# Two transformer blocks in one kernel: four of the six modulation vectors summed by POOL from two ring slots of their own, the in-projection on six slots, retention outputs finished tile by tile

## The chip, the cores and the metric

The kernel runs on one NeuronCore of a Trainium2 chip. The engines that matter are TensorE (PE, matrix products and transposes), VectorE (DVE), ScalarE (ACT), GpSimd (POOL) and SyncE (SP, which here issues weight loads). The metric is device microseconds of one launch, the median of several runs; lower is better.

## What is computed

Two blocks follow each other on 256 tokens of width 1024, everything in float32. The change touches the first one, and in it the vectors that modulate the norms, the projections and the retention heads:

```python
mod = silu(cond) @ w_mod + b_mod          # 1024 x 6144, six vectors of 1024 (shift1, scale1, gate1, shift2, scale2, gate2)
h  = rms_norm(x) * (1 + mod[1]) + mod[0]
hc = rms_norm(ctx) * (1 + mod_c[1]) + mod_c[0]
rq, rk, rv, rg, dq, dk, dv = split(h @ w_in)            # and the same of hc for keys and values
ret  = rms_norm(retention(rq, rk, rv)) * silu(rg)       # 4 heads, decaying scores
diff = rms_norm(differential_attention(dq, dk, dv))     # 4 heads, two softmaxes each
x  = x + mod[2] * (concat(ret, diff) @ w_out)
h2 = rms_norm(x) * (1 + mod[4]) + mod[3]
x  = x + mod[5] * peer_ffn(h2)   # per token 8 x 16 of 16384 experts are looked up and gathered
```

Only the first two vectors are needed for the context too (`mod_c`). The other four are needed for the latent tokens alone. The second block (block attention, a gated delta rule, a mixture of experts) comes behind all of this and is not changed.

## The kernel before

One function, `two_blocks`, writes a program for each engine by hand, with semaphores between them. All weights of the first block come in chunks of 1 MB (128 partitions x 2048 floats, seen as 8 feature blocks `k` of 256 columns) through a ring `wring` of 8 slots. Chunk `n` lives in slot `n % 8`; SP issues its load as soon as chunk `n - 8` was used (`chunk_used`), strictly in the order of `n`. The order of the stream is: 8 chunks of modulation vectors 0 and 1 (4 chunks for each vector), 12 of the in-projection, 12 of the vectors 2 to 4, then 4 of the out-projection (with those of vector 5 in between), 9 of the peer queries and their keys. The first expert gathers follow.

What happens, in order:

- **In-projection.** PE works through 19 parts (`IN1_PARTS`, each 32 matmuls of `L2344` in the trace's count), because 7 of the 12 chunks are used for the latent and for the context tokens. From part 10 on (`HEADS_FROM`), `diff_heads(p)` puts one piece of the eight differential-attention heads ahead of each part: the transposed heads (`L2275`), two score products (`L2286`), the transposes of the softmaxed rows of the head before (`L637`), and the outputs of the one before that (`L2304`). For each head DVE takes the row maxima (`L1499`, `L1500`), ACT the exponentials (`L905`), and DVE combines the two softmaxes (`L1503`, `L1504`, `L1508`, the last one over 128x512). Between these DVE also writes the decay tables (`L1486` to `L1493`) and rotates queries and keys (`rope`, `L1455` to `L1465`). Ahead of head 0 and of head 4 PE waits for the semaphore `roped`, which DVE raises behind its rotations (`L1469`, `L1561`).
- **Modulation vectors 2 to 4.** For each vector `mod_products` (`L620`) multiplies four chunks by the silu of the condition: four groups of rows in PSUM, 64 matmuls. ACT copies the result to `mod_rows` (`L879`), `mod_turn` (`L630`) adds the four groups and turns the row into a column by 8 tiny matmuls, and DVE adds the bias (`modulation`, `L1363`). These stand between the retention work: `scores(h)` (`L2363`), the masked decay by DVE (`mask_scores`, `L1544`), `outputs(h)` (`L2375`), which writes both token tiles of a head and raises `ret_y`.
- **Norms and out-projection.** ACT squares the outputs of a tile (`ret_squares`, `L931`), takes a root (`L939`), DVE normalizes (`L1531` to `L1536`), PE transposes the tile (`turn_mixed`), `project_out(t)` (`L2414`, 128 matmuls) multiplies it with the four out-projection chunks, DVE adds the gated result to x (`add_mixed`, `L1599`). Tile 0 goes first; `project_out(1)` stands behind the first two peer queries. The vector 5 is multiplied on PE ahead of the first query.
- **Peer experts.** A query (`L2441`) and its key scores (`L2455`) give DVE 16 experts per head and token; POOL gathers their rows from HBM (`L787`, 256 gathers of 1 MB into a ring of 8 places `G`), DVE takes the dot products (`L1809`), PE adds the weighted rows (`weighted_rows`, `L2478`), which frees a place (`slot_used`). POOL has no other work ahead of the first gather. Its few tensor operations (`mask_level`, `L807`, and `L822` to `L831`) come in the second block.

## Time and profile before

| What | Value |
|---|---|
| three runs, us | 1366.46, 1367.21, 1372.5; median 1367.21 |
| span of the profiled execution, us | 1367.2 |
| PE busy | 1162.8 us, 85% of the span |
| DVE busy | 713.7 us, 52% |
| ACT busy | 392.0 us, 29% |
| POOL busy | 286.6 us, 21% |
| transfers | 446.79 MB, mean 327 GB/s |
| first gather starts | 269.16 us |

No own time of the profiled execution is listed beside its span. The span agrees with the median of the runs to 0.01 us, so sums made against the span can be read as sums against the median. The span falls into three stages: up to some 270 us the first block's attention, up to some 925 us the gathers, and then the second block.

### The profile page before, as it was taken

Reading aid. Unit: us, or ns where it says so; the run is one execution under the profiler, and the core shown is the slowest. Engines: PE = TensorE matmul, PEld = TensorE weight load, DVE = VectorE, ACT = ScalarE, POOL = GpSimd, SP = SyncE. Lnnn points to the kernel's source line nnn. Section 1 sums busy time; section 2 is a strip of 40 time slices with the busy share of each in tenths; the row PEclk is TensorE's granted clock in tenths of the full one; section 3 lists DMA queues with packets and bytes.
Section 4 is the critical chain, followed back from the end, with each engine's and each line's share of the span. In section 5 each row is a group of like instructions: output and inputs, shape, how many; then the busy total and the mean of one; then the engine's idle time right before and its main releaser. Section 6 shows DMA issues by size and latency. Waiting matters only on the chain.

```text
span 1367.2 us, 16345 instructions
## 1 busy us (share of the span) xinstructions
PE 1162.8 (85%) x5986; PEld 716.0 (52%) x5986; DVE 713.7 (52%) x1850; ACT 392.0 (29%) x1094; POOL 286.6 (21%) x275
## 2 busy tenths in 40 slices
PE   6999998989999987778777777778999998867896
PEld 4887877874555532223222223325978875332342
DVE  2365532487677777767777666644752515311112
ACT  2203532223333333333233334222531423000011
POOL 0000000024444444444444434440030000000000
PEclk9999999999999999999999999999999998999999
DMA  9711237399999999999999999997521474999996
GB/s 392 302 62 62 93 116 315 147 406 395 421 421 421 422 420 421 422 421 399 422 422 422 421 419 399 421 422 313 196 94 63 185 292 177 427 424 424 425 388 257
DMA packets 60283, 446.79 MB, mean 327 GB/s; under 512 B 6704, under 2 KB 7088, under 8 KB 10160
## 3 DMA queue, kind: packets, MB, share of 16 engines
q0 software_dynamic: 36864, 268.45, 47.5%
q1 hardware_dynamic: 22912, 175.97, 31.8%
q10 hardware_dynamic: 432, 1.40, 0.3%
q8 instruction: 44, 0.72, 0.2%
q14 instruction: 31, 0.25, 0.0%
HBM read 444.74 MB, written 1.05 MB: 326 GB/s over the span
## 4 chain that ended last, share of the span: by engine, by line
PE 52%; DMA 34%; DVE 6%; ACT 4%; issue 2%; SPq 0%; POOL 0%; DVEq 0%; ACTq 0%
DMA arena<-uv_in,arena 26%; PE bank L2478 12%; PE bank L2344 9%; DMA wring<-moe_in 4%; PE bank L2575 4%; PE bank L2821 3%; PE bank L2441 3%; PE bank L2837 2%; DMA wring<-stream_in 2%; DVE arena L1809 2%; PE bank L2780 2%; DMA arena<-moe_in 2%; PE bank L2572 2%; PE bank L2807 2%; PE bank L637 1%
## 5 line engine op out<-in xcount | busy, mean ns | idle before, releaser
L2478 PE MATMUL bank<-arena 128*128 128x512 f32 x1024 | 474.1, 606 | 116.9 <-ACT arena L1069 116.9
L1809 DVE CUSTOM_DVE_ANT_0 arena<-arena 128x1024 f32<-128x1024 f32 x256 | 314.0, 1226 | 192.5 <-DMA arena<-uv_in,arena 191.5
L787 POOL DMA_INDIRECT arena<-uv_in,arena x256 | 272.0, 1063 | 650.1 <-PE bank L2478 365.7
L2478 PEld LDWEIGHTS bank<-arena 128*128 128x128 f32 x1024 | 186.6, 191 | 374.3 <-ACT arena L1069 192.7
L1061 ACT ACTIVATE arena<-arena 128x2 f32<-128x2 f32 x128 | 26.2, 205 | 410.0 <-DVE arena L1809 409.8
L2344 PE MATMUL bank<-wring,arena 128*128 128x256 f32 x608 | 134.1, 381 | 1.0 <-DVE arena L1384 1.0
L2344 PEld LDWEIGHTS bank<-wring,arena 128*128 128x128 f32 x608 | 115.2, 191 | 17.7 <-DVE arena L1384 1.1
L1069 ACT ACTIVATE arena<-const,arena 128x128 f32<-128x128 f32 x256 | 86.7, 385 | 0.0
L2441 PEld LDWEIGHTS bank<-arena,wring 128*128 128x128 f32 x384 | 57.0, 196 | 20.2 <-issue 15.3
L2821 PE MATMUL bank<-arena 128*32 128x512 f32 x288 | 59.7, 616 | 7.5 <-DMA arena<-moe_in 4.9
L2821 PE MATMUL bank<-wring,arena 128*32 128x512 f32 x288 | 59.7, 620 | 7.2 <-DMA wring<-moe_in 7.2
L2441 PE MATMUL bank<-arena,wring 128*128 128x128 f32 (+1 forms) x384 | 63.4, 314 | 1.8 <-DMA wring<-stream_in 1.8
L1065 ACT ACTIVATE arena<-arena 128x1 f32<-128x1 f32 x256 | 61.4, 287 | 4.2
L2575 PE MATMUL bank<-arena,wring 128*128 128x256 f32 x256 | 57.3, 381 | 0.0
L2575 PEld LDWEIGHTS bank<-arena,wring 128*128 128x128 f32 x256 | 48.0, 190 | 7.2 <-issue 0.8
L2162 DVE TENSOR_TENSOR arena<-bank,arena 128x256 f32<-128x256 f32 x9 | 3.8, 425 | 89.3 <-ACT arena L1294 89.3
L2837 PE MATMUL bank<-arena 128*32 128x512 f32 x184 | 34.6, 626 | 11.4 <-DMA wring<-moe_in 5.5
L2843 PE MATMUL bank<-arena 128*128 128x512 f32 x72 | 33.4, 604 | 8.6 <-DVE arena L2176 7.0
L2807 PEld LDWEIGHTS bank<-arena 128*128 128x128 f32 x288 | 34.8, 201 | 10.6 <-issue 8.0
L2807 PE MATMUL bank<-arena 128*128 128x128 f32 x288 | 36.3, 287 | 4.1 <-DVE arena L2064 4.1
L960 ACT ACTIVATE arena<-bank 128x512 f32<-128x512 f32 x19 | 11.3, 597 | 93.7 <-PE bank L2344 93.7
L620 PE MATMUL bank<-wring,tiny 128*32 128x256 f32 x384 | 26.2, 423 | 10.3 <-DMA wring<-stream_in 10.3
(458 smaller groups left out, 1318.5 us busy)
## 6 DMA issues: line engine op xcount, KB each, us to landing
wring<-stream_in SPq DMA_DIRECT2D x67, 1024.0 KB, 8.9
wring<-moe_in SPq DMA_DIRECT2D x14, 2048.0 KB, 17.9
arena<-moe_in SPq DMA_DIRECT2D x26, 1024.0 KB, 17.7
arena<-moe_in SPq DMA_DIRECT2D x12, 2048.0 KB, 18.7
wring<-moe_in SPq DMA_DIRECT2D x13, 1024.0 KB, 14.2
arena<-uv_in,arena POOLq DMA_INDIRECT x256, 12.8
arena<-moe_in SPq DMA_DIRECT2D x4, 512.0 KB, 10.7
wring<-moe_in SPq DMA_DIRECT2D x4, 512.0 KB, 11.2
```

The lines of the kernel that those rows point to most:

```text
L787: pool.indirect_dma_start(G[:, j, :], None, uv_d, src).then_inc(gathered[j], 16)
L1065: nc.scalar.activation(weight[:, at + q:at + q + 1], gelu[:, at + q:at + q + 1], ACT.Copy, scale=gates[:, first + q:first + q + 1]).then_i ...
L1069: nc.scalar.activation(diag[:, at + q, :], ident, ACT.Copy, scale=weight[:, at + q:at + q + 1]).then_inc(diag_ready, 1)
L1809: v.tensor_tensor_reduce(out=junk, in0=G[:, j, 0:D], in1=h2[:, t, :], scale=1.0, scalar=0.0, op0=ALU.mult, op1=ALU.add, accum_out=dots[:, ...
L2344: ins = mm(bank[1 + q % 2][:, t * COLS:(t + 1) * COLS], h[:, k, t * P:(t + 1) * P], w[:, k, :], start=k == 0, stop=k == KD - 1)
L2441: ins = mm(out[:, j, cols], w[:, k, j * P:(j + 1) * P], h2T[:, k, cols], start=k == 0, stop=k == KD - 1)
L2478: ins = mm(bank[1 + 2 * tile + c][:, :], diag[:, j, :], G[:, j, D + c * 512:D + (c + 1) * 512], start=False, stop=False, skip_group_check= ...
L2575: ins = mm(out[:, j * T:(j + 1) * T], w[:, k, j * P:(j + 1) * P], h3T[:, k, :], start=k == 0, stop=k == KD - 1)
L2807: ins = mm(bank[1 + k // 4][:, (k % 4) * P:(k % 4 + 1) * P], h4[:, t, k * P:(k + 1) * P], hotx[:, t], start=t == 0, stop=t == NT - 1)
L2821: ins = mm(bank[0][ROWS * j:ROWS * (j + 1), :], XT[:, k, ROWS * j:ROWS * (j + 1)], gu_buf(s)[:, k, :], start=k == 0, stop=k == KD - 1)
L2837: ins = mm(bank[1 + h][ROWS * j:ROWS * (j + 1), :], hidT[:, f, ROWS * j:ROWS * (j + 1)], home[:, f, h * 512:(h + 1) * 512], start=f == 0, ...
L2843: return mm(bank[4 + 2 * t + h][:, :], comb[:, t * P:(t + 1) * P], Yx[:, h * 512:(h + 1) * 512], start=False, stop=False, skip_group_check ...
```

## The change

The vectors 2 to 5 ("late" ones, 16 chunks) leave PE's products. POOL gets a loop ahead of its gathers: for each late chunk it multiplies 8x256 weights by the condition in place, and adds 4 blocks to 4, 2 to 2 and 1 to 1; the last addition writes 256 columns of `mod_rows`. PE only turns the row, with a matrix of ones, which sums over partitions too; the waits are on the new semaphore `pool_done`, raised four times for a chunk. The late chunks have slots 6 and 7 of the ring for themselves. The 12 in-projection chunks share slots 0 to 5, and the out-projection begins at slot 0 again. SP issues a late load behind certain in-projection loads (`LATE_MODS_AFTER`) and waits there for POOL, the last two behind the load of the keys.

On PE `mod_turn(2)` goes ahead of part 9, `mod_turn(3)` behind the fourth head's piece, `mod_turn(4)` behind the last part. DVE's `modulation(2)` moves ahead of the first `roped`, `modulation(3)` behind head 3's rows, `modulation(4)` ahead of the masked scores. The outputs of retention heads 2 and 3 are done for tile 0 first and then for tile 1. `project_out(1)` is cut into chunk 0, the sums of the norm, chunk 1, and later chunks 2 and 3, into banks 1 and 2; `clear(1)` and `clear(2)` now wait until DVE has read them.

```diff
+LATE_MODS_AFTER = {C_IN1 + 2: (0,), C_IN1 + 3: (1,), C_IN1 + 6: (2, 3), C_IN1 + 7: (4,), C_IN1 + 8: (5, 6),
+                   C_IN1 + 9: (7, 8), C_IN1 + 10: (9,), C_IN1 + 11: (10, 11, 12, 13), C_SK: (14, 15)}
@@ PE mod_turn
-            pe.wait_ge(mod_out, 2 * g + (1 if half == 0 else 2))
-            pe.wait_ge(cond_pick, 2)
+            if g < 2:
+                pe.wait_ge(mod_out, 2 * g + (1 if half == 0 else 2))
+                pe.wait_ge(cond_pick, 2)
+            else:
+                pe.wait_ge(pool_done, POOL_STEPS * MOD_GROUP * (g - 1))
@@ SP
+            def late_mod_in(m):
+                s = late_mod_slot(m)
+                if m < 2:
+                    sp.wait_ge(chunk_used, C_IN1 - 1 + m)
+                else:
+                    sp.wait_ge(pool_done, POOL_STEPS * (m - 1))
...
-                sp.wait_ge(chunk_used, n + 1 - WSLOTS)
+                if C_OUT1 <= n < C_IN2 and s >= IN1_SLOTS:
+                    sp.wait_ge(pool_done, POOL_STEPS * (LATE_MODS - WSLOTS + 1 + s))
+                else:
+                    sp.wait_ge(chunk_used, last_chunk_in(s, n) + 1)
@@ POOL, ahead of the gathers
+            for m in range(LATE_MODS):
+                g, n = 2 + m // MOD_GROUP, m % MOD_GROUP
+                w = slot_view(late_mod_slot(m))
+                pool.wait_ge(chunk_here[late_mod_slot(m)], 16 * (m // 2 + 2))
+                nc.gpsimd.tensor_tensor(w, w, bc(condS[:, :, 0], 2, COLS), ALU.mult).then_inc(pool_done, 1)
+                pool.wait_ge(pool_done, POOL_STEPS * m + 1)
+                nc.gpsimd.tensor_tensor(w[:, 0:4, :], w[:, 0:4, :], w[:, 4:8, :], ALU.add).then_inc(pool_done, 1)
+                pool.wait_ge(pool_done, POOL_STEPS * m + 2)
+                nc.gpsimd.tensor_tensor(w[:, 0:2, :], w[:, 0:2, :], w[:, 2:4, :], ALU.add).then_inc(pool_done, 1)
+                pool.wait_ge(pool_done, POOL_STEPS * m + 3)
+                if n == 0:
+                    pool.wait_ge(mod_turned, g + 1)
+                nc.gpsimd.tensor_tensor(mod_rows[:, n * COLS:(n + 1) * COLS], w[:, 0, :], w[:, 1, :], ALU.add)
@@ ACT
-            modulation_out(2, (6, 3))
-            modulation_out(3, (6, 3))
-            modulation_out(4, (1, 2))
-            modulation_out(5, (1, 2))
-                act.wait_ge(ret_y, RH)
+                act.wait_ge(ret_y, RH - 1 + t)
@@ PE, in-projection and retention
+                if q == HEADS_FROM - 1:
+                    mod_turn(pe, 2)
+                elif q == HEADS_FROM + 3:
+                    mod_turn(pe, 3)
...
-            mod_products(pe, 2, (6, 3))
-            outputs(0)
+            outputs(0).then_inc(ret_y, 1)
...
-            outputs(2)
-            mod_products(pe, 3, (6, 3))
-            outputs(3)
-            mod_turn(pe, 3)
-            mod_products(pe, 4, (1, 2))
+            outputs(2, (0,))
+            outputs(3, (0,)).then_inc(ret_y, 1)
+            outputs(2, (1,))
+            outputs(3, (1,)).then_inc(ret_y, 1)
...
-            mod_products(pe, 5, (1, 2), (0, 1))
+            project_out(1, (0,))
             sums_over_features(pe, sq2[0], 1, second=2)
-            mod_products(pe, 5, (1, 2), (2, 3))
+            project_out(1, (1,))
...
-            project_out(1)
+            project_out(1, (2, 3))
+            pe.wait_ge(x2_ready, 3)
             clear(1)
```

POOL before, at the head of its program; each row is one instruction or several alike, with the semaphores that it waits for:

```order
L783 UNCONDITIONAL_BRANCH [waits barrier_Pool_Activation_PE_DVE_SP_gather]
L787 DMA arena<-uv_in,arena 128x2048 [waits first_here]
L787 DMA arena<-uv_in,arena 128x2048 x7
L787 DMA arena<-uv_in,arena 128x2048 [waits slot_used,top_ready]
L787 DMA arena<-uv_in,arena 128x2048 [waits slot_used] x7
```

And after (the four tensor operations of the first chunk; 60 more follow ahead of the gathers):

```order
L832 UNCONDITIONAL_BRANCH [waits barrier_Pool_Activation_PE_DVE_SP_gather]
L843 ISA
L843 TENSOR_TENSOR wring<-wring,tiny 128x2048 [waits chunk_here6,inputs_ready]
L845 TENSOR_TENSOR wring<-wring 128x1024 [waits pool_done]
L847 TENSOR_TENSOR wring<-wring 128x512 [waits pool_done]
L851 TENSOR_TENSOR mod_rows<-wring 128x256 [waits mod_turned,pool_done]
```

The gathers now stand behind 64 tensor operations.

PE before, from the end of the in-projection (the last `L2344`) into the retention; `bank6<-wring,tiny` is `mod_products` of vector 2:

```order
L2344 MATMUL bank1<-wring,arena 128x256 x15
L2304 MATMUL bank7<-arena 128x128 [waits diff_aT_out]
L2304 MATMUL bank7<-arena 128x128 x3
L2363 MATMUL bank4<-arena 128x256 [waits proj_out,diff_exp,turned_out,const_here]
L2363 MATMUL bank4<-arena 128x256
L2363 MATMUL bank5<-arena 128x256 x2
L2363 MATMUL bank1<-arena 128x256 x2
L2363 MATMUL bank2<-arena 128x256 x2
L620 MATMUL bank6<-wring,tiny 32x256 [waits chunk_here4,diff_aT_out]
L620 MATMUL bank6<-wring,tiny 32x256 x7
```

And after, from the same place (`L664` is `mod_turn`, `L2442` are `outputs`):

```order
L2410 MATMUL bank1<-wring,arena 128x256 x15
L664 MATMUL bank3<-const,mod_rows 128x2 [waits pool_done,turned_out]
L664 MATMUL bank3<-const,mod_rows 128x2 x7
L2366 MATMUL bank7<-arena 128x128 [waits diff_aT_out]
L2366 MATMUL bank7<-arena 128x128 x3
L2430 MATMUL bank4<-arena 128x256 [waits diff_exp,proj_out,const_here]
L2430 MATMUL bank4<-arena 128x256
L2430 MATMUL bank5<-arena 128x256 x2
L2430 MATMUL bank1<-arena 128x256 x2
L2430 MATMUL bank2<-arena 128x256 x2
L2442 MATMUL bank0<-arena 128x128 [waits diff_y_out,ret_masked,diff_aT_out]
```

The products are gone and a turn stands in front.

DVE before, the rotation of the second tile and the first `roped`, on which PE's head 0 waits:

```order
L1455 TENSOR_TENSOR arena<-arena,const 128x1024 [waits dve_step]
L1462 TENSOR_TENSOR arena<-arena,const 128x32x16 x2
L1465 TENSOR_TENSOR arena<-arena 128x1024 [waits dve_step]
L1469 MEMSET tiny 128x128 [waits dve_step]
L1476 COPY arena<-bank 128x512 [waits turned] x2
```

And after (`L1424` is `modulation(2)`):

```order
L1516 TENSOR_TENSOR arena<-arena,const 128x1024 [waits dve_step]
L1523 TENSOR_TENSOR arena<-arena,const 128x32x16 x2
L1526 TENSOR_TENSOR arena<-arena 128x1024 [waits dve_step]
L1424 TENSOR_TENSOR tiny<-bank,small 128x16 [waits mod_turned,dve_step]
L1531 MEMSET tiny 128x128 [waits dve_step]
L1538 COPY arena<-bank 128x512 [waits turned] x2
```

One wait for PE's turn came in ahead of `roped`.

## Rows read from the trace of the kernel before

**Rows 1.** The page: DMA share of the span's 40 equal slices, in tenths.
```profile
DMA  9711237399999999999999999997521474999996
```
**Rows 2.** Chain that ended last, 0 to 360: start, duration, what.
```profile
221.53 9.04 DMA wring<-stream_in
...
249.72 4.89 DMA wring<-stream_in
```
**Rows 3.** Stretches: length, busy of PE, PEld, DVE, ACT, POOL, clock, DMA share, GB/s.
```profile
262.00:269.00 7.00, 6.48 (x58) 6.32 (x57) 6.38 (x33) 2.99 (x5) 0.00 (x0) 1.00 0.03 9
...
305.00:311.00 6.00, 4.57 (x14) 2.23 (x13) 5.79 (x18) 2.70 (x11) 2.37 (x2) 1.00 0.78 289
...
500.00:600.00 100.00, 73.70 (x160) 28.60 (x159) 69.72 (x178) 32.15 (x109) 41.02 (x40) 1.00 1.01 421
```
**Rows 4.** PE in order of time, 60 to 330: start, duration, line, idle before.
```profile
187.16 7.07 PE L2344 MATMUL bank<-wring,arena 128*128 128x256 f32 x32
...
197.98 3.66 PE L620 MATMUL bank<-wring,tiny 128*32 128x256 f32 x64
...
205.48 1.95 PE L630 MATMUL bank<-tiny,mod_rows 128*128 128x2 f32 x16
...
216.74 2.05 PE L2375 MATMUL bank<-arena 128*128 128x128 f32 x16
...
226.59 1.07 PE L637 MATMUL bank<-const,arena 128*128 128x128 f32 x8
230.71 17.08 PE L2414 MATMUL bank<-arena,wring 128*128 128x128 f32 x128 [3.05 <-DMA wring<-stream_in]
...
255.92 3.84 PE L2441 MATMUL bank<-arena,wring 128*128 128x128 f32 x32 [1.56 <-DMA wring<-stream_in]
...
267.00 14.46 PE L2414 MATMUL bank<-arena,wring 128*128 128x128 f32 x128
...
288.25 3.76 PE L608 MATMUL bank<-arena,const 128*128 128x128 f32 x16 [5.07 <-ACT arena L993]
```
**Rows 5.** DVE and POOL in order of time around 1011 to 1021.
```profile
1011.25 0.69 DVE L1917 TENSOR_TENSOR arena<-arena 128x512 f32<-128x512 f32 x1 [2.70 <-ACT arena L1188]
1011.29 1.77 POOL L807 TENSOR_TENSOR arena<-arena 128x512 f32<-128x512 f32 x1 [58.14 <-ACT arena L1188]
1012.04 1.57 DVE L1918 TENSOR_TENSOR arena<-arena 128x512 f32<-128x512 f32 x1
...
1014.78 1.90 POOL L822 TENSOR_TENSOR arena<-arena 128x1024 f32<-128x1024 f32 x1 [1.72 <-ACT arena L1196]
...
1018.59 0.42 DVE L1927 TENSOR_TENSOR arena<-arena,bank 128x256 f32<-128x256 f32 x1
...
1021.08 1.26 POOL L831 TENSOR_TENSOR arena<-arena 128x512 f32<-128x512 f32 x1
```
**Rows 6.** DVE in order of time: the two roped, one head's rows, one norm.
```profile
102.95 0.17 DVE L1469 MEMSET tiny<- 128x128 f32 x1
...
114.38 0.75 DVE L1508 SCALAR_TENSOR_TENSOR arena<-arena,tiny 128x512 f32<-128x512 f32 x1
...
144.13 0.17 DVE L1561 MEMSET tiny<- 128x128 f32 x1
...
222.62 0.69 DVE L1536 TENSOR_TENSOR arena<-arena 128x512 f32<-128x512 f32 x1
```
**Rows 7.** PE in order of time: where it needs those results of DVE.
```profile
105.32 1.04 PE L2275 MATMUL bank<-const,arena 128*128 128x128 f32 x8
...
119.41 0.66 PE L637 MATMUL bank<-const,arena 128*128 128x128 f32 x4
...
145.71 0.60 PE L2275 MATMUL bank<-const,arena 128*128 128x128 f32 x4
```
**Rows 8.** POOL in order of time: the first and the ninth gather.
```profile
269.16 1.12 POOL L787 DMA_INDIRECT arena<-uv_in,arena  x1 [268.73 <-DVE arena L1702]
...
299.12 0.96 POOL L787 DMA_INDIRECT arena<-uv_in,arena  x1 [20.15 <-PE bank L2478]
```

More of the change, by code:

```diff
@@ L46 @@
 C_IN1 = 2 * MOD_GROUP
-C_OUT1 = C_IN1 + N_IN1 + 4 * MOD_GROUP
+C_OUT1 = C_IN1 + N_IN1
 C_Q = C_OUT1 + N_OUT
@@ L50 @@
 C_IN2 = C_Q + N_Q + N_SK
-C_MOD = [0, MOD_GROUP] + [C_IN1 + N_IN1 + i * MOD_GROUP for i in range(4)]
+C_MOD = [0, MOD_GROUP]
 C_OUT2 = C_IN2 + N_IN2
@@ L55, with chunk_slot, late_mod_slot, chunk_turn @@
 WSLOTS = 8
+LATE_MODS = 4 * MOD_GROUP
+IN1_SLOTS = 6
+POOL_STEPS = 4
+MODS_SUMMED = POOL_STEPS * LATE_MODS
+def chunk_slot(n):
+    if C_IN1 <= n < C_OUT1:
+        return (n - C_IN1) % IN1_SLOTS
+    if C_OUT1 <= n < C_IN2:
+        return (n - C_OUT1) % WSLOTS
+    return n % WSLOTS
+def late_mod_slot(m):
+    return IN1_SLOTS + m % 2
+def chunk_turn(n):
+    late = LATE_MODS // 2 if n >= C_OUT1 and chunk_slot(n) >= IN1_SLOTS else 0
+    return late + sum(chunk_slot(m) == chunk_slot(n) for m in range(n + 1))
+LATE_MODS_AFTER = {C_IN1 + 2: (0,), C_IN1 + 3: (1,), C_IN1 + 6: (2, 3), C_IN1 + 7: (4,), C_IN1 + 8: (5, 6),
+                   C_IN1 + 9: (7, 8), C_IN1 + 10: (9,), C_IN1 + 11: (10, 11, 12, 13), C_SK: (14, 15)}
 SM = {}
@@ L185, in last_chunk_in @@
 def last_chunk_in(slot, before):
-    return max(n for n in range(before) if n % WSLOTS == slot)
+    return max(n for n in range(before) if chunk_slot(n) == slot)
 def two_blocks(nc, xT_d, ctxT_d, small_d, rows_d, const_d, masks_d, wstream_d, gate2_d, uv_d, route_d,
@@ L625, in mod_turn @@
         def mod_turn(pe, g, half=None):
[L627 to L628 removed]
+            if g < 2:
[3 more added lines that the diff above has]
+                pe.wait_ge(pool_done, POOL_STEPS * MOD_GROUP * (g - 1))
             for k in range(KD) if half is None else range(4 * half, 4 * half + 4):
                 ins = nc.tensor.matmul(bank[MOD_BANK[g] if half != 1 else 5][:, 2 * k:2 * k + 2],
[L631 removed]
+                                       mod_rows[:, k * P:(k + 1) * P], pick[:, 0:2] if g < 2 else ones[:, 0:2],
+                                       start=True, stop=True)
             ins.then_inc(mod_turned, 1)
@@ L787, in gather @@
                 pool.indirect_dma_start(G[:, j, :], None, uv_d, src).then_inc(gathered[j], 16)
+            pool.wait_ge(inputs_ready, 1)
+            for m in range(LATE_MODS):
[10 more added lines that the diff above has]
+                    pool.wait_ge(mod_turned, g + 1)
+                nc.gpsimd.tensor_tensor(mod_rows[:, n * COLS:(n + 1) * COLS], w[:, 0, :], w[:, 1, :], ALU.add)\
+                  .then_inc(pool_done, 1)
             pool.wait_ge(first_here, 1)
@@ L2349, in _ @@
                     ins.then_inc(chunk_used, 1)
+            pe.wait_ge(turned_out, len(sources))
+            mod_turn(pe, 4)
             diff_heads(DH * NT + 1)
             pe.wait_ge(const_here, 32)
-            pe.wait_ge(turned_out, len(sources))
             pe.wait_ge(proj_out, len(IN1_PARTS))
@@ L2365, in scores, with outputs @@
                 ins.then_inc(ret_scores, 1)
-            def outputs(h):
+            def outputs(h, tiles=range(NT)):
                 pe.wait_ge(ret_masked, h + 1)
@@ L2370, in outputs @@
                     pe.wait_ge(diff_y_out, NT)
-                for t in range(NT):
+                for t in tiles:
                     for k in range(4):
@@ L2404, in turn_mixed, with project_out @@
                         .then_inc(mixT_done, 1)
-            def project_out(t):
+            def project_out(t, chunks=range(N_OUT)):
                 pe.wait_ge(mixT_out, 2 * t + 2)
-                for n in range(N_OUT):
+                for n in chunks:
                     chunk_ready(pe, C_OUT1 + n)
```

59 lines of the change are left out of this document (29 added, 30 removed).

## The prediction, made before the changed kernel was run

> **What bounds the kernel now.** I read the page first. The DMA row of its slices is full from the eighth slice (some 270 us) to the twenty-seventh (some 925 us), and low before [rows 1]. The stretches say what that means: in 500 to 600 us the DMA share is 1.01 at 421 GB/s while PE idles a quarter of the time; just ahead of the first gather it is 0.03 [rows 3]. So the gather stage is a block of fixed length that is paid from the first gather on, at 269.16 us [rows 8], and the second block hangs behind it. What this change can move is the date of the first gather. Ahead of it the chain of waits is PE nearly throughout, with two pieces of weight loads: 9.04 us at 221.53 and 4.89 us at 249.72 [rows 2]. The PE timeline shows them as idle times of 3.05 and 1.56 us [rows 4]. POOL is idle all this time, 268.73 us ahead of its first gather [rows 8].
>
> **What goes away, part by part.** One group of products (64 matmuls) is 3.66 us, one turn 1.95 us [rows 4]. Three groups between 195 and 231 us go. Their turns do not go: two move into the in-projection, one to its end, so PE pays them there, less overlaps some 1.7 us each, 5 us together. Before, the retention from the end of the in-projection (187.16 + 7.07 = 194.2) to the last output (216.74 + 2.05 = 218.8) takes 24.6 us [rows 4], of which two groups and a turn are about 9.0. The rest, 15.6, stays. Since tile 0 is now finished first, its outputs end some 2 us earlier, and DVE's mask of head 3 is then about 0.5 late. So tile 0 is ready 5.0 + 15.6 - 2.0 + 0.5 = 19.1 us behind the old 194.2, at 213.3 instead of 218.8. From there the squares, the root and DVE's norm take as before: from 218.8 to 222.62 + 0.69 = 223.3 [rows 6], 4.5 us. PE turns the tile at 217.8 instead of 226.59, and the out-projection starts behind turn and copy (2.3 us) at 220.1 instead of 230.71: the 3.05 us of waiting for its weights are gone, since their loads are now issued during the in-projection. That is 10.6 us so far.
>
> Between the starts of `project_out(0)` and `query(0)` there were 25.2 us. Half a group of products twice (3.7) and the load wait of 1.56 go, two quarters of `project_out(1)` come in, each 14.46 / 4 = 3.6 [rows 4], and the first of them waits some 1 us for the copied tile. 25.2 - 5.2 + 7.2 + 1.0 = 28.2, so 3.0 us are given back, and a last 0.3 for the norm's row behind the later sums. The first gather comes 7.3 us earlier. Slots 6 and 7 don't delay the queries: with free engines the sixteenth late chunk is summed by about 225 us, and query 1 needs slot 6 some 20 us later.
>
> Behind the first gather DVE's selection for two heads sets `add_mixed(1)`; it shifts alike. New is that `clear` waits for it. The clears used to lie in a PE gap that ends with 5.07 us of waiting at 288.25, where the sums took 3.76 us instead of 2.05 [rows 4]. Now they and the sums start late together; I take 0.3 us. Two of the four query loads that ran beside the first gathers come earlier now, 2.1 MB or 5.0 us at 421 GB/s. I count nothing for it: the ninth gather is held by PE until 299.12 [rows 8], and the DMAs already have a hole behind it, share 0.78 in 305 to 311 [rows 3]. The hole gets larger instead; at most those 5 us are a gain. ACT's copies of the products go too; they hid beside PE and are worth nothing. **Without a cost of POOL's work: 1367.2 - 7.0 = 1360.2.**
>
> **What it adds.** No tensor operation of POOL runs in this stage before, so I bound it. The nearest rows: 1.26 us for two full operands of 512, 1.90 for 1024 with a broadcast factor [rows 5]. Doubling by size, a chunk is 3.8 + 2.5 + 1.3 + 0.6 = 8.2 us, and sixteen are 131 us. That fits between 38 us (first late chunk landed) and the gather at 262. The order that PE's turns impose splits it: chunks 0 to 4 from 38 to about 80, a pause until `mod_turn(2)` at 100 because `mod_rows` is still full, then 5 to 8, a short pause until `mod_turn(3)`, 9 to 12, a pause until `mod_turn(4)`, and 13 to 15.
>
> The question is what this does to DVE. In the only place where both read SBUF [rows 5], POOL's operation at 1011.29 took 1.77 us instead of 1.26, and DVE's at 1012.04 took 1.57 instead of 0.69, ending 0.55 us behind POOL's, about what its own data phase takes. That is full blocking in both directions, one behind the other. DVE's operation at 1018.59, which has one input in PSUM, ran its 0.42 us beside POOL unhindered. The Trainium skill (page "SBUF — State Buffer", section "Who interferes with whom") says this as a rule: a DVE instruction with two SBUF inputs and a GpSimd instruction that reads SBUF exclude each other for the whole instruction. It speaks against the change; by it the sum is the one below, and by a rule that shared the bandwidth instead it would be near the 1360 above.
>
> So each DVE operation with two SBUF inputs may wait for a whole POOL operation, 0.6 to 3.8 us, and POOL's next one then takes its turn ahead of DVE's next. In each head's part of 9 to 10 us DVE has 5 to 6 of them (`L1504`, `L1508`, the decay and rope lines), and PE leaves little room: `L1508` of head 0 ends at 115.1 and PE needs it at 119.41, 4.3 us; the second `roped` is at 144.3 and PE needs it at 145.71, 1.4 us; the first at 103.1 against 105.32, 2.2 us plus 1.7 of the inserted turn [rows 6, 7]. I walked through the parts, alternating the two engines:
> - first `roped`: POOL restarts at 100 with 0.6, 3.8, 2.5 us between DVE's last rope operations, and DVE arrives there some 2 us late; 113 against 107.4: 5.6 us.
> - heads 0 and 1: `L1504` and `L1508` wait behind 2.5 and 1.3 us, and the decay table of head 0 pushes the maxima of head 1: 0.3 and 3.2 us.
> - head 3 and the second rope, six operations beside chunk 9: `roped` 5.1 us late at head 4.
> - heads 4 and 5, decay sums and tables beside chunks 11 and 12: PE late by 3.0 and 2.1 us.
> - tail: the norm's product of tile 0 (`L1536`) meets chunk 13 or 14: 1.3 us.
>
> The sum is 20.6 us, beside 131 us of POOL work that could block at most. **1360.2 + 20.6 = 1380.8.** The lower end is 0, if every wait falls into slack; the upper end I take at 33, where chunk 1 also delays the context rows (`L1404`, 3 us of room there) and the three weak places come twice as bad.
>
> **The rivals.**
> - *The cover holds.* DVE is busy for hardly more than half of a part, POOL's pauses fall on its tight stretches, so PE never waits: 1360.2, down to 1357 if the two early loads count too. For it: POOL waits from about 80 to 100, just while DVE normalizes and rotates. Against it: 1.4 us of room at 145. This ends on the other side, and decides from the point where PE's added waits stay under 7 us. Chance 0.20.
> - *Half of it.* Blocking is real, but DVE's linked operations slip in before POOL's next one is issued, so a pair waits once instead of twice: some 10 us, 1370. Chance 0.22.
> - *POOL is late itself.* If an operation there took twice as long (262 us together), the turns and then the first gather would wait for POOL's chunk 15: chunks 13 to 15 alone would end 49 us after `mod_turn(4)`, near 252, still ahead of the gather, but `mod_turn(2)` and `mod_turn(3)` would hold PE some 10 and 20 us: 1390 and more. With everything above 1393: chance 0.08.
> - The forecast, blocking in alternation, 1372 to 1393: chance 0.50.
>
> The Trainium skill (page "GPSIMD Engine Reference", section "Performance versus the Vector engine") gives 4497 ns for an addition of 2048, where twice-doubled 1.26 us gives 5.0; the multiplication with its broadcast factor has no figure there. It would make a chunk about 8.4 us and change nothing above.
>
> **How the numbers follow.** The predicted time is the likeliest case's, 1380.5. The range 1359 to 1393 leaves out the low part of the first rival (under 0.10) and the 0.08 above. A measurement of this kernel can tell about 0.5% or 6.8 us from no change. Faster than 1360.4 is only a little more than half of the first rival: 0.13. Within 0.5%, up to 1374, are the rest of it, most of the half case and a little of the forecast: 0.30. Slower: 0.57.
>
> **What would show it.** Of the step on PE: no `L620` behind 195 us, no idle time for stream loads, and `project_out(0)` starting 23 to 25 us behind the end of the in-projection instead of 36.5. Of POOL: 8.2 us a chunk, pauses at the three turns, all done by 260. Of the blocking: `L1508`, `L1493` and the rope lines with means of 1.5 to 3 us instead of 0.4 to 0.75, PE idle behind DVE in front of the heads by some 19 us in sum, and the last part of the in-projection ending near 217 instead of 194. It would be wrong if those DVE means hardly rise, or if they rise and PE still runs through; then the gather starts near 262 instead of 282.

## The result, and the profile after

| | before | after |
|---|---|---|
| median of the runs | 1367.64 us (1366.46 to 1372.5) | 1391.58 us (1390.0 to 1393.06) |
| ratio after / before | | 1.0169, 95% interval 1.0143 to 1.0195 |
| span of the profiled execution | 1367.2 us | 1390.6 us |
| first gather starts | 269.16 us | 295.68 us |

The changed kernel is 24 us slower; 13.3 were forecast. The page of the changed kernel shows where. Its DMA row (40 slices of the span) is full from the eleventh slice on; the row of before was full from the ninth [rows 1]:

```profile
DMA  9723342268999999999999999997631364999996
```

The block of gathers has kept its length: from the first gather on there were 1367.2 - 269.16 = 1098.0 us before, and there are 1390.6 - 295.68 = 1094.9 now. So the loss, 26.5 us, lies wholly ahead of the first gather, and some 3 us come back behind it.

POOL in order of time (start, duration, engine, line; in brackets the idle time before it and what ended it): the four operations of the first late chunk, the three pauses that PE's turns impose, and the first gather. In the kernel before, that gather was the first thing POOL did [rows 8]:

```profile
43.55 3.62 POOL L843 TENSOR_TENSOR wring<-wring,tiny 128x2048 f32<-128x2048 f32 x1 [43.12 <-DMA wring<-stream_in]
47.25 2.35 POOL L845 TENSOR_TENSOR wring<-wring 128x1024 f32<-128x1024 f32 x1
49.68 1.26 POOL L847 TENSOR_TENSOR wring<-wring 128x512 f32<-128x512 f32 x1
51.02 2.65 POOL L851 TENSOR_TENSOR mod_rows<-wring 128x256 f32<-128x256 f32 x1
...
110.95 1.17 POOL L851 TENSOR_TENSOR mod_rows<-wring 128x256 f32<-128x256 f32 x1 [25.32 <-PE bank L664]
...
160.44 0.72 POOL L851 TENSOR_TENSOR mod_rows<-wring 128x256 f32<-128x256 f32 x1 [13.97 <-PE bank L664]
...
231.76 0.72 POOL L851 TENSOR_TENSOR mod_rows<-wring 128x256 f32<-128x256 f32 x1 [36.68 <-PE bank L664]
...
295.68 1.12 POOL L836 DMA_INDIRECT arena<-uv_in,arena  x1 [37.88 <-DVE arena L1764]
```

POOL is not late: it waits 76.0 us in three pauses for PE and 37.9 us for the gather's indices. VectorE (DVE) is late. Its groups of instructions between 20 and 300 us (line, shape, count, then busy time, mean of one in ns, and idle time before them):

```profile
L1445 DVE TENSOR_SCALAR arena<-arena,tiny 128x256 f32<-128x256 f32 x16 | 19.0, 1256 | 0.1
L1548 DVE TENSOR_SCALAR arena<-const,tiny 128x512 f32<-128x512 f32 x4 | 6.6, 1661 | 0.1
L1561 DVE TENSOR_REDUCE tiny<-bank 128x1 f32<-128x512 f32 x16 | 10.9, 683 | 8.9 <-PE bank L2348 8.9
L1570 DVE SCALAR_TENSOR_TENSOR arena<-arena,tiny 128x512 f32<-128x512 f32 x8 | 13.7, 1710 | 0.3
L1606 DVE SCALAR_TENSOR_TENSOR arena<-bank,arena 128x512 f32<-128x512 f32 x8 | 5.1, 685 | 6.7 <-PE bank L2430 6.7
```

and the same groups of the kernel before:

```profile
L1384 DVE TENSOR_SCALAR arena<-arena,tiny 128x256 f32<-128x256 f32 x16 | 5.4, 409 | 0.1
L1486 DVE TENSOR_SCALAR arena<-const,tiny 128x512 f32<-128x512 f32 x4 | 1.9, 484 | 0.1
L1499 DVE TENSOR_REDUCE tiny<-bank 128x1 f32<-128x512 f32 x16 | 11.0, 687 | 14.9 <-PE bank L2286 14.9
L1508 DVE SCALAR_TENSOR_TENSOR arena<-arena,tiny 128x512 f32<-128x512 f32 x8 | 6.0, 752 | 0.3
L1544 DVE SCALAR_TENSOR_TENSOR arena<-bank,arena 128x512 f32<-128x512 f32 x8 | 5.1, 684 | 3.5 <-PE bank L2363 3.5
```

The multiply-add of two SBUF tiles (`L1570`, before `L1508`) takes 1710 ns instead of 752. The forms that read PSUM (`bank`, `L1561` and `L1606`) are as they were: they are the control. But the scaling of the hidden rows (`L1445`) and the decay arguments (`L1548`) are three times as long too, and they have only one tile of SBUF as input, beside factors of one column each. The mean of 1256 ns still hides the size of it: eight of the sixteen scalings, those of the context rows, take 16.28 us together from 53.12 us on, and took 2.68 before; the other eight ran before POOL started and are unchanged.

What of this reaches PE stands in the table of its waits up to the first gather (line, releaser, sum, times, longest):

```profile
PE bank L651 <- DMA wring<-stream_in: 9.9, 3, 9.0
PE bank L2337 <- DVE tiny L1625: 7.3, 1, 7.3
PE bank L2410 <- DVE arena L1445: 6.4, 5, 2.9
PE bank L672 <- DVE arena L1570: 5.7, 2, 4.9
PE bank L672 <- DVE arena L1598: 4.8, 1, 4.8
PE bank L2348 <- ACT arena L970: 2.0, 1, 2.0
```

### The profile page after: what moved, and what is told of

It is laid out like the page before. It is cut to its first block, busy times and chain, and to the rows that moved or that the text cites. A ratio compares the mean times of both kernels' runs of the same rounds, so it can differ in the third digit from the quotient of the medians.

```text
span 1390.6 us, 15886 instructions
## 1 busy us (share of the span) xinstructions
PE 1163.1 (84%) x5730; PEld 712.0 (51%) x5730; DVE 783.6 (56%) x1850; ACT 388.3 (28%) x1086; POOL 426.6 (31%) x339
## 2 busy tenths in 40 slices
DMA packets 60282, 446.77 MB, mean 321 GB/s; under 512 B 6704, under 2 KB 7088, under 8 KB 10160
## 4 chain that ended last, share of the span: by engine, by line
PE 48%; DMA 33%; DVE 11%; ACT 5%; issue 3%; SPq 0%; DVEq 0%; ACTq 0%
DMA arena<-uv_in,arena 26%; PE bank L2538 12%; PE bank L2410 6%; PE bank L2881 4%; PE bank L2635 4%; DMA wring<-moe_in 4%; PE bank L2501 3%; PE bank L2840 2%; DVE arena L1871 2%; DMA wring<-stream_in 2%; PE bank L2897 2%; PE bank L2475 2%; DMA arena<-moe_in 2%; PE bank L2632 2%; PE bank L2867 1%
## 5 line engine op out<-in xcount | busy, mean ns | idle before, releaser
L2538 PE MATMUL bank<-arena 128*128 128x512 f32 x1024 | 478.5, 611 | 111.6 <-ACT arena L1130 111.1
L836 POOL DMA_INDIRECT arena<-uv_in,arena x256 | 277.2, 1083 | 412.8 <-PE bank L2538 363.6
L2410 PE MATMUL bank<-wring,arena 128*128 128x256 f32 x608 | 140.9, 391 | 7.2 <-DVE arena L1445 6.4
L843 POOL TENSOR_TENSOR wring<-wring,tiny 128x2048 f32<-128x2048 f32 x16 | 59.2, 3702 | 43.1 <-DMA wring<-stream_in 43.1
L845 POOL TENSOR_TENSOR wring<-wring 128x1024 f32<-128x1024 f32 x16 | 39.6, 2473 | 1.3
```

The costliest lines, as they stand in the source:

```text
L836: pool.indirect_dma_start(G[:, j, :], None, uv_d, src).then_inc(gathered[j], 16)
L843: nc.gpsimd.tensor_tensor(w, w, bc(condS[:, :, 0], 2, COLS), ALU.mult).then_inc(pool_done, 1)
L2410: ins = mm(bank[1 + q % 2][:, t * COLS:(t + 1) * COLS], h[:, k, t * P:(t + 1) * P], w[:, k, :], start=k == 0, stop=k == KD - 1)
L2538: ins = mm(bank[1 + 2 * tile + c][:, :], diag[:, j, :], G[:, j, D + c * 512:D + (c + 1) * 512], start=False, stop=False, skip_group_check= ...
```

## The experiments

Each kernel but one starts from the changed one. The date of the first gather is the measure in all of them: what follows it is of nearly fixed length, 1094.9 to 1099.4 us in the profiled execution of every kernel whose mixture of experts loads as much as before. The edits are shown in extracts: the signals (`.then_inc`) are left out, and so are most of the waits between POOL's steps.

**Without the sums.** Is it POOL's work, or the waits, slots and orders that came with it?

```
- nc.gpsimd.tensor_tensor(w, w, bc(condS[:, :, 0], 2, COLS), ALU.mult)
+ nc.gpsimd.memset(w[:, 0, 0:8], 0.0)
...
- nc.gpsimd.tensor_tensor(mod_rows[:, n * COLS:(n + 1) * COLS], w[:, 0, :], w[:, 1, :], ALU.add)
+ nc.gpsimd.memset(mod_rows[:, n * COLS:(n + 1) * COLS], 0.0)
```

> The changed kernel, but each of the 64 POOL operations that sum the sixteen late chunks (3.62, 2.35, 1.26 and 0.72 us) is replaced by a small memset that only writes (8 columns, the last one 256). Left out by this: the sums of modulation vectors 2 to 5, which become their bias alone. Kept: every load, every slot, every wait and semaphore, PE's turns, the order of SP, PE and VectorE. Theory A (VectorE's operations with both inputs in SBUF wait while POOL's sums run, nothing else of the change costs anything): this is the prediction's sum without POOL, 1360.2 us, within 1356 to 1364; project_out(0) starts at about 233 (255.6 in the changed kernel, 230.7 before less 10.6 plus what the first turn gives), the first gather near 262; the context rows' scaling (L1445) takes 0.41 us for 128x256 again, the head parts' multiply-add (L1570) 0.75 us. Rival B (the new waits and places - six slots, output tiles in another order, POOL's turn waits - cost the time): it stays between 1380 and 1392, the head parts as late as in the changed kernel.

Measured: first gather at 263.2 us, 32.5 earlier than in the changed kernel. The time, 1391.49 us, lies outside theory A's range, and does not show this: with other modulation vectors the tokens choose other experts in the second block's mixture, 453.06 MB are moved instead of 446.77, and the part behind the first gather takes 1127.6 us instead of 1094.9. So rival B's number came out and its mechanism did not. The scaling is at 410 ns again and the multiply-add at 752; taken by the date, the sums are the whole loss. (The expectation's 233 for `project_out(0)` was a slip: it starts at 222.42.) PE's stretch up to the first gather (length, busy with count for PE, PEld, DVE, ACT, POOL, granted clock, DMA share, GB/s), of the changed kernel and of this one:

```profile
0.00:295.68 295.68, 253.33 (x1436) 211.31 (x1437) 181.37 (x260) 74.69 (x152) 134.94 (x69) 0.93 0.45 177
```
```profile
0.00:263.20 263.20, 242.41 (x1436) 205.94 (x1437) 111.26 (x260) 74.06 (x152) 10.00 (x68) 0.97 0.49 198
```

Both hold the same 1436 matmuls. PE's idle time is 295.68 - 253.33 = 42.35 us in the one and 20.79 in the other: **21.6 us are waits**. The rest, 253.33 - 242.41 = **10.9 us, is the same work at a slower clock** (mean 0.93 instead of 0.97). It isn't POOL's traffic that slows the matmuls: from 75 to 86 us, at a granted clock of 1.00 and with POOL busy for 10.3 of the 11 us, the changed kernel runs 53 matmuls of 379 ns each, as many and as long as the kernel before with POOL idle. From 150 to 200 us, for example, of the changed kernel and of this one:

```profile
150.00:200.00 50.00, 40.69 (x202) 32.95 (x203) 36.36 (x38) 15.20 (x28) 33.77 (x16) 0.90 0.42 159
```
```profile
150.00:200.00 50.00, 49.20 (x262) 40.68 (x261) 22.28 (x48) 24.11 (x47) 0.94 (x8) 1.00 0.39 155
```

A mean of 0.90 is a mix of the clock's two levels, 2.4 and 1.2 GHz; where PE had stood idle for DVE it was granted the lower one for a part of the time.

**POOL busy, but only writing.** Seven memsets a chunk (two each of 2048, 1024 and 512 columns, one of 256), without a read:

```
- nc.gpsimd.tensor_tensor(w, w, bc(condS[:, :, 0], 2, COLS), ALU.mult)
...
+ for dst in (w, w, w[:, 0:4, :], w[:, 0:4, :], w[:, 0:2, :], w[:, 0:2, :]):
+     nc.gpsimd.memset(dst, 0.0)
+ nc.gpsimd.memset(mod_rows[:, n * COLS:(n + 1) * COLS], 0.0)
```

> The changed kernel, but POOL is kept as busy by seven memsets a chunk (twice 2048 columns, twice 1024, twice 512, once 256), which write SBUF and read nothing. Left out: the sums of modulation vectors 2 to 5, which become their bias. Same loads, slots and turns. Theory A1 (what holds VectorE up is POOL reading SBUF): VectorE's operations keep the durations of the kernel before (L1570 0.75 us, L1487 form 0.48, L1445 0.41) and the time is that of the kernel without sums, 1356 to 1364. Theory A2 (what holds it up is any POOL instruction under way): the same operations are as long as in the changed kernel wherever a memset runs, and the time lies above 1370, by as much as POOL's busy time per chunk comes to 8.2 us. Theory A3 (only the forms that an own port pair serves at a faster rate wait for a writer): the tensor_scalar forms (L1445, L1548) are longer, the tensor_tensor and multiply-add ones are not; then 1362 to 1370.

Measured: first gather at 259.8 us (and, with the same longer rest, 1389.83 us). The memsets keep POOL busy for 111.1 us up to the gather, a little less than the 134.9 of the sums. DVE's groups here; `L1441` is the hidden rows' scaling, `L1544` the decay arguments, `L1566` the multiply-add, `L1522` the addition of the rotation, `L1472` and `L1473` the small operations of the decay constants:

```profile
L1441 DVE TENSOR_SCALAR arena<-arena,tiny 128x256 f32<-128x256 f32 x16 | 10.6, 730 | 0.1
L1472 DVE TENSOR_TENSOR tiny<-tiny 128x8 f32<-128x8 f32 x7 | 1.2, 167 | 0.2
L1473 DVE TENSOR_SCALAR tiny<-tiny 128x8 f32<-128x8 f32 x7 | 6.5, 932 | 0.2
L1522 DVE TENSOR_TENSOR arena<-arena 128x512 f32<-128x512 f32 x2 | 1.4, 692 | 0.1
L1544 DVE TENSOR_SCALAR arena<-const,tiny 128x512 f32<-128x512 f32 x4 | 6.2, 1544 | 0.1
L1566 DVE SCALAR_TENSOR_TENSOR arena<-arena,tiny 128x512 f32<-128x512 f32 x8 | 6.0, 752 | 0.3
```

Theory A3 has the mechanism: while POOL only writes, the operations with two inputs run free, and the tensor_scalar forms still wait. Theory A1 has the date: a first gather no later than without POOL's work, so the waits of the tensor_scalar forms alone fall into slack here. The Trainium skill (page "SBUF — State Buffer", section "Who interferes with whom") has both: beside the two-input rule it says that `tensor_scalar` can enter a 2-port mode and then excludes GpSimd, and that a `tensor_reduce` never does on trn2. The trace agrees: the tensor_scalar of 512 columns, at 484 ns before faster than a tensor_tensor of the same size at 692, takes 1544 beside the memsets, and in the kernel below that starts its sums behind the context rows a tensor_reduce that reads 1024 columns of SBUF beside them keeps its 1.22 us.

**The same sums in pieces of 256 columns**, 15 operations a chunk instead of four:

```
+ for k in range(KD):
+     ins = nc.gpsimd.tensor_tensor(w[:, k, :], w[:, k, :], condS[:, k, 0:1].to_broadcast([P, COLS]), ALU.mult)
+ ins.then_inc(pool_done, 1)
```

> The changed kernel with the same sums, but POOL's operations are cut into pieces of 256 columns: 8 multiplies, 4 adds, 2 adds and 1 add a chunk instead of one of each; results and waits are the same. Theory A (a VectorE operation that meets a POOL operation waits until that one instruction has ended, then runs, then POOL waits for it in turn): the longest wait falls from 3.6 to at most 0.75 us, the mean of L1445, L1570, L1526 comes nearer to the kernel before (L1570 below 1.2 us), and 12 to 18 us of the 31 between the changed kernel and its cover come back: 1372 to 1379. Rival C (the two engines share the path in small turns, so what counts is the work that POOL does, not the length of its instructions): VectorE's means stay as they are, the time stays at 1385 to 1395 or above, as POOL's busy time grows by the fixed part of each instruction.

Measured: 1367.79 us, ratio to before 0.9998 (0.9976 to 1.002), first gather at 268.3. Theory A, and by more than it said (23.8 us came back, 12 to 18 were expected). POOL does more (180.8 us up to the gather instead of 134.9), and yet PE's idle time shrinks to 268.3 - 244.1 = 24.2 us, about that of the kernel without sums and one wait of 3.8, for the first rotated rows:

```profile
L1576 DVE SCALAR_TENSOR_TENSOR arena<-arena,tiny 128x512 f32<-128x512 f32 x8 | 9.3, 1168 | 0.3
```
```profile
PE bank L2343 <- DVE tiny L1537: 3.8, 1, 3.8
```

The multiply-add waits 0.42 us on average (1168 - 752) instead of 0.96: what a DVE operation pays is the rest of one POOL instruction, so the length of POOL's instructions counts and not their sum. Rival C, by which POOL's total would count, is out.

**The sums at other times.** POOL's chunk 0 waits for the decay constants, chunks 2 to 9 for one more finished head part each; turns, bias additions and loads follow later (`mod_turn(4)` behind the first mixed tile, and into another bank).

```
+ if m == 0: pool.wait_ge(gam_ready, 1)
+ elif 2 <= m < 10: pool.wait_ge(lam_dots, m)
- if q == HEADS_FROM - 1: mod_turn(pe, 2)
- elif q == HEADS_FROM + 3: mod_turn(pe, 3)
+ if q == HEADS_FROM + 3: mod_turn(pe, 2)
+ elif q == HEADS_FROM + 7: mod_turn(pe, 3)
```

> The changed kernel with the same sums at other times: POOL's chunk 0 waits until the decay constants are made (behind the context rows' scaling), chunks 2 to 9 wait each for one more head part of the eight to have ended on VectorE, PE's turns and VectorE's additions of the bias follow later (vector 2 in head part 3, vector 3 in head part 7, vector 4 behind the first mixed tile), and SP issues the later chunks' loads behind other weights. So the first eight sums spread out, and eight of the sixteen run behind the heads, where few VectorE operations have both inputs in SBUF. Theory A (collisions are the cost; fewer of them on PE's path give back the time): context rows at 0.41 us, head parts with at most one chunk each, 1366 to 1376. Rival D (moving the sums moves the collisions and adds waits at the turns): 1378 to 1392; PE would then stand idle in front of a turn (L664) or in front of the first mixed tile's use of vector 2.

Measured: 1364.03 us, ratio 0.9959 (0.9939 to 0.9979), first gather at 264.1. Theory A, a little better than its range. The same POOL instructions, 131.7 us of them, cost PE next to nothing:

```profile
0.00:264.10 264.10, 243.64 (x1436) 206.93 (x1437) 135.49 (x268) 74.50 (x152) 131.66 (x69) 0.97 0.51 198
```
```profile
L1574 DVE SCALAR_TENSOR_TENSOR arena<-arena,tiny 128x512 f32<-128x512 f32 x8 | 15.1, 1884 | 0.3
```

The multiply-add is even longer than in the changed kernel (1884 ns), and PE waits 0.3 us for it. The mean of a group says whether there is blocking, not whether it costs anything. The longest wait of PE for DVE is 3.1 us, in front of the mixed tile (2.7 without sums). Run again without an edit:

> The gated kernel once more, without any edit, against the kernel before, to narrow its interval. Expected: 1362 to 1366 us, ratio 0.995 to 0.998. If it was luck of one series, the ratio is 0.998 to 1.002.

Measured: 1365.62 us, ratio 0.9976 (0.9961 to 0.9992). Both intervals lie under 1, so the gain (0.41% and 0.24%) is likely real, but it is less than the 0.5% that the prediction took as the limit of what can be told.

**The start of the sums alone.** POOL waits until the last context row is scaled, and starts at 53.4 us instead of 43.6:

```
+ pool.wait_ge(h_ready, 2 * KD)
  for m in range(LATE_MODS):
```

> The changed kernel with one wait more: POOL's first sum starts when VectorE has scaled the last context row (near 60 us instead of 43.6). Everything else, the whole instructions of 2048, 1024, 512 and 256 columns too, stays. Theory A (each stretch of VectorE work pays for the POOL work that lies over it): the context rows come back to 0.41 us each and PE's waits for them (6.4 us in the changed kernel, 1.0 without sums) go, with part of the slower clock; POOL is then still at its chunks between 86 and 111 us, where it stood idle before, and its operations meet the normalising and rotating of the first rows, which ran free; that delays the first turned heads by 3 to 6 us. So the first gather comes 2 to 8 us earlier than the changed kernel's 295.7, at 288 to 294, and the time is 1384 to 1390. Rival E (the context rows are the root, and all the later waits follow from PE being late there): the first gather at 275 or earlier, the time under 1373.

Measured: 1406.18 us, ratio 1.0279 (1.0254 to 1.0304), first gather at 304.6: **later by 8.9 us**, where theory A gave 2 to 8 us earlier and rival E 20. Both were wrong. PE waits 1.0 us for the context rows, as hoped, and then

```profile
PE bank L2338 <- DVE tiny L1532: 26.1, 1, 26.1
```

for the first rotated rows. POOL's second chunk and then DVE in order of time show how they go in step; the small operations of the decay constants took 0.17 us each before:

```profile
61.62 3.62 POOL L844 TENSOR_TENSOR wring<-wring,tiny 128x2048 f32<-128x2048 f32 x1
65.31 2.36 POOL L846 TENSOR_TENSOR wring<-wring 128x1024 f32<-128x1024 f32 x1
67.75 1.28 POOL L848 TENSOR_TENSOR wring<-wring 128x512 f32<-128x512 f32 x1
69.11 0.74 POOL L852 TENSOR_TENSOR mod_rows<-wring 128x256 f32<-128x256 f32 x1
```
```profile
61.72 3.54 DVE L1477 TENSOR_TENSOR tiny<-tiny 128x8 f32<-128x8 f32 x1
65.29 0.17 DVE L1478 TENSOR_SCALAR tiny<-tiny 128x8 f32<-128x8 f32 x1
65.50 2.20 DVE L1477 TENSOR_TENSOR tiny<-tiny 128x8 f32<-128x8 f32 x1
67.73 0.17 DVE L1478 TENSOR_SCALAR tiny<-tiny 128x8 f32<-128x8 f32 x1
67.94 1.12 DVE L1477 TENSOR_TENSOR tiny<-tiny 128x8 f32<-128x8 f32 x1
69.09 0.17 DVE L1478 TENSOR_SCALAR tiny<-tiny 128x8 f32<-128x8 f32 x1
69.29 0.57 DVE L1477 TENSOR_TENSOR tiny<-tiny 128x8 f32<-128x8 f32 x1
```

An operation of 8 columns lasts exactly until POOL's instruction ends (61.62 + 3.62 = 65.24), whether that is 3.6 or 0.7 us; the next one slips in before POOL has started again, and the one after waits for the whole of POOL's next. A row of short, linked operations so takes as long as the POOL instructions beside it: from the third of the constants' operations to the last, 24.7 us instead of 4.5.

**Constants or rotation?** The same, but POOL starts when the constants are made (`gam_ready`), 6 us later.

> The changed kernel, but POOL's first sum starts only when VectorE has made the decay constants (some 6 us later than in the kernel that waits for the context rows, near 60 us). In that kernel the constants' small operations took up to 3.5 us each, yet 19.65 us of idle time stood behind them in the kernel before, while the row of normalising and rotating operations of the first rows (24.4 us long before, 2.3 us ahead of PE) took 54 us. Theory A (what counts is the row of operations with two SBUF inputs that PE waits for; the constants had slack): the constants are at 0.17 us each again, the rotation is as late as before, PE waits 20 to 27 us in front of the first turned heads, the first gather at 298 to 306, the time 1397 to 1408. Rival I (the constants' delay was on the path): the first gather at 280 to 292, the time under 1390.

Measured: 1407.61 us, ratio 1.0291 (1.0267 to 1.0315), first gather at 309.3. Theory A: the time is at the upper end of its range, the first gather 3.3 us behind it, and PE waits 28.9 us for the first rotated rows where 20 to 27 were expected. The constants are at 0.17 us each again and it helps nothing, because behind them DVE idles; the normalising and rotating, with POOL now beside all of it, lasts from 78.71 to 136.03 us. Before it began at 78.59 and was done at 102.95 [rows 6]:

```profile
78.71 1.27 DVE L1494 TENSOR_TENSOR arena<-arena 128x1024 f32<-128x1024 f32 x1 [19.64 <-ACT arena L1026]
...
95.92 4.53 DVE L1505 TENSOR_TENSOR arena<-arena,tiny 128x1024 f32<-128x1024 f32 x1
...
136.03 0.17 DVE L1532 MEMSET tiny<- 128x128 f32 x1
```

The changed kernel owed it to luck that it lost only 26.5 us: it ran its sums over the context rows and stood in its first pause, 85.6 to 111 us, just while DVE normalised and rotated, so that the same operations took 0.68 to 1.23 us each from 89.1 to 110.9 us.

**Start and pieces, and gates and pieces.**

> The changed kernel with the wait for the last context row and the pieces of 256 columns. The kernel with pieces alone has its first gather at 268.3, where PE still waited 3.8 us for the second rotated rows and had a clock of 0.92 between 75 and 120 us. Theory A: with the context rows already cheap in pieces (0.59 us instead of 0.41, PE waited no longer there), the added wait gives nothing but shifts POOL's work later: first gather 266 to 270, time 1364 to 1370. Rival G (POOL's sums in that early stretch cost PE's clock): the first gather under 265.

Measured: 1376.99 us, ratio 1.0064 (1.0043 to 1.0085), first gather at 280.3, 12 us behind the kernel with pieces alone (whose wait of 3.8 us, said above to be for the second rotated rows, was for the first). Neither: PE now waits for POOL, twice, in front of a turn (first row below). Of the 12 us PE is idle for 4.7; for the other 7.3 it is busy with the same 1436 matmuls, at a mean clock of 0.93 instead of 0.96.

> The kernel with the gated sums (first gather at 264.1, 0.9 us behind the one without sums at 263.2) and the pieces of 256 columns in one. Theory A (nearly all that waits on PE's path is gone with the gates, and the pieces only shorten waits that are hidden now): the first gather at 262 to 265, the time within 0.3% of the gated kernel's, 1360 to 1366. Rival F (POOL's longer busy time with pieces, 0.74 us for 256 columns where a 2048-column instruction took 3.7, makes its last chunk or a turn late): 1366 to 1372, with PE idle in front of a turn.

Measured: 1372.81 us, ratio 1.004 (1.0027 to 1.0053), first gather at 272.8. Rival F, by the same wait (second row), a little above its range. Against the gated kernel PE is idle 3.5 us longer and busy 5.2:

```profile
PE bank L664 <- POOL mod_rows L858: 7.6, 2, 5.0
```
```profile
PE bank L665 <- POOL mod_rows L862: 4.5, 2, 4.2
```

Pieces cost POOL 165.0 us up to the gather in the second kernel, where whole instructions took 131.7; a late start or gates leave no room for that before the turns. The two remedies don't add up.

**POOL's reads alone, in the kernel before.**

```
+ pool.wait_ge(x_here, 32)
+ for i in range(104):
+     nc.gpsimd.tensor_tensor(spare, bc(ident, 1, 4), bc(ident, 1, 4), ALU.add)
```

> The kernel before with 104 POOL additions of 512 columns, one after the other from about 20 us on, both inputs and the output in SBUF and the result used by nobody; all the rest, its loads, slots and PE's sums, as before. By the changed kernel's 1.26 us for such an addition they take 131 us and more where VectorE takes its turns. Theory A (POOL reading SBUF is enough to hold VectorE up, with nothing of the change there): VectorE's operations with SBUF inputs up to some 155 us get longer by up to 1.3 us each, the tensor_scalar forms too, the ones that read PSUM do not; the first gather moves from 269.2 to 273 to 280 and the time to 1371 to 1378. Rival H (the slots and the new order are needed for the loss): no change, 1366 to 1369.

Measured: 1391.15 us, ratio 1.0165 (1.0136 to 1.0193), first gather at 293.4. Theory A's mechanism, at some three times its price: with nothing of the change in it, this kernel is as slow as the changed one. Against 248.41 us busy and 20.8 idle before, PE has 33.2 us idle here and 11.8 more busy. That the loss is as large as the changed kernel's is chance, since this kernel keeps the PE work that the change takes away, and has other POOL instructions:

```profile
0.00:293.40 293.40, 260.18 (x1628) 212.82 (x1629) 153.51 (x261) 78.68 (x160) 124.38 (x109) 0.93 0.43 171
```
```profile
PE bank L2282 <- DVE tiny L1476: 12.2, 1, 12.2
```

I had reckoned with waits of at most 1.3 us each, but not with nearly all operations of the normalising and rotating meeting one: from 95.5 us on those of 512 columns took 1.41 to 1.52 us instead of 0.69. So POOL's additions are enough, without the slots, waits and orders of the change; rival H is out.

## Why the prediction was right, and where its size was off

- **The gather stage has a fixed length, only its start moves:** right, 1098.0 against 1094.9 us.
- **What goes away, 7.3 us up to the gather without POOL's cost:** right, 6.0 measured. The kernel without sums has its first gather at 263.2; 261.9 was forecast. Its in-projection ends at 192.19 + 7.07 = 199.3 (with the two turns inside it, 194.2 + 2 x 1.7 = 197.6 forecast) and `project_out(0)` starts at 222.42 (220.1 forecast). No wait for stream loads is left there.

```profile
192.19 7.07 PE L2410 MATMUL bank<-wring,arena 128*128 128x256 f32 x32
...
222.42 17.04 PE L2475 MATMUL bank<-arena,wring 128*128 128x128 f32 x128 [0.69 <-ACT arena L1048]
```

- **POOL's 8.2 us a chunk:** right, 3.62 + 2.35 + 1.26 + 0.72 and the gaps; 59.2 + 39.6 + 21.3 + 15.2 = 135.3 us in all. It starts at 43.6, not 38, resumes at 111, not 100, and is done at 257.8, before the 260 forecast.
- **Full blocking in alternation:** right, and in both directions: the addition of 256 columns at 51.02 lasts 2.65 us instead of 0.72, since a DVE operation of 2048 columns runs from 50.36 to 53.09. It is shown three ways: it goes when the sums go, it comes with POOL's additions alone, and its waits shrink with the pieces. "Half of it" and "POOL is late itself" fell (POOL itself became late only where I cut its instructions up).
- **Which operations:** the step that failed in kind. The prediction counted those with two SBUF inputs. The tensor_scalar forms wait as well, and the first to do so were the scalings of the context rows (`L1445`), which I had not counted. I had the context rows only at the range's upper end and by the two-input operation ahead of the scalings (`L1404`), which now takes 2.73 us instead of 2.29. PE waited 5.4 us more for the scaled rows.
- **The sum of PE's waits, 20.6 us:** 21.6 measured, but by offsetting errors.

| place | forecast | measured |
|---|---|---|
| context rows | 0 | 5.4 |
| first rotated rows | 5.6 | 0: ready at 117.71, just before PE came at 117.76, itself 9.2 us later than without sums |
| heads 0 to 2, multiply-add | 3.5 | 4.9 |
| second rotated rows | 5.1 | 7.3 |
| heads 4 to 7 | 5.1 | 2.0, in front of a result of ACT |
| norm of tile 0 | 1.3 | 2.1 |

- **What was mis-sized: the clock, 0 against 10.9 us.** The forecast took each wait of PE at its face value. The same 1436 matmuls took 253.33 us instead of 242.41. The other differences nearly cancel: 1.3 us less was saved up to the gather, the waits were 1.0 longer, and 3.4 more came back behind it. So this term makes the gap between the forecast and the 1390.6 of the profiled execution. (The forecast's last step has a slip too: the sum is 1380.8, and 1380.5 was given.) Some of it may be chance: the first 50 us had a granted clock of 0.90 to 0.97 in the profiled executions of different kernels, and the kernel with memsets, at 0.97 there, ran the 1436 matmuls in 238.31 us. So the term is uncertain by about 4 us. Nor does it follow the waits in proportion: against the kernel without sums it was 3.6 us in the one that starts behind the context rows (245.98 us busy at 37.8 us of added waits), 6.6 in the one behind the constants, and 9.0 in the one with start and pieces, at 8.1 us of added waits. In the first of these the granted clock was 0.66 from 100 to 135 us, but only 8.9 us of work lay in that stretch; in the kernel before with POOL's additions it was 0.73 from 225 to 250 us, with 24.3 us of work in it, long after POOL's last addition. What decides it stays open.
- **The signs in the changed kernel itself:** the in-projection ended at 229.9 us, not near 217, and `project_out(0)` started 25.7 us behind it, where 23 to 25 were forecast. Of the means, `L1508` (now `L1570`, 1.71 us) and the rotation's additions (`L1526`, 2.87 and 2.34) rose as forecast, the decay sum `L1493` (now `L1555`) only from 0.68 to 0.82. PE stood idle in front of the heads for 12.2 us more instead of some 19, since the first rotated rows and heads 4 to 7 cost less than forecast. The reading of the DMA row before was off by one slice: it is full from the ninth.
- **Behind the gather:** 0.3 us were forecast as a loss, up to 5.0 as a gain not counted. 3.1 came back. The kernels with gates, with the same work there, came to 1097.6 and 1099.4 in two executions, and the others with the changed order to 1095.9 to 1098.3, so this is hardly told apart from scatter.

The account of the profiled executions: 1367.2 - 6.0 (PE's busy time, 248.41 to 242.41) + 21.6 + 10.9 - 3.1 = 1390.6.

## What to carry to other kernels

Before work is given to an idle POOL, look at what VectorE does beside it. Here its instructions with two inputs in SBUF, and the tensor_scalar forms wider than one column, waited for the rest of the whole POOL instruction that they met. So count VectorE's instructions on the path, each with up to the length of a POOL instruction, and not busy times. Place the sums where VectorE reads PSUM or idles, or cut them up if POOL has time to spare, and judge moved work by the path, since a start 10 us later cost 15 us more here. And price waits of TensorE above their length: in the kernels where it waited 8 us more or longer, a further 3.6 to 11.8 us went to the slower clock, though not in proportion.

## What the runs showed that I had not expected

- A tensor_scalar with one SBUF tile waits for POOL, also when POOL only writes (730 instead of 409 ns for 128x256, 1544 instead of 484 for 128x512); a tensor_tensor, even of 8 columns, only when POOL reads (up to 3.54 us instead of 0.17). A tensor_reduce out of SBUF stayed at 1.22 us for 128x1024 between operations that took up to 4.35, in the kernel that starts behind the context rows.
- Of the operations of a single column, the tensor_scalar stayed at 154 ns in the changed kernel, while the scalar_tensor_tensor rose from 219 to 940.
- Where VectorE did not hold it, POOL took 0.72 us for an addition of 256 columns, 2.35 for 1024, and 3.62 for the multiplication of 2048 by one factor a block.
